# Gate and up products of two feed-forward blocks: the weights' high part times both parts of x in one product of 512 columns

## What is computed

```python
D_FF = 2816
def swiglu(x, w_gate, w_up, w_down):
    return (jax.nn.silu(x @ w_gate) * (x @ w_up)) @ w_down
...
    for l in range(DEPTH_2):
        h = x + 0.5 * swiglu(rms_norm_2(x, ffn1_norm[l]), ffn1_gate[l], ffn1_up[l], ffn1_down[l])
        u = rms_norm_2(h, mix_norm[l])
        ...
        h = h + jnp.concatenate([y_da, y_sc, y_lru], axis=-1) @ w_out[l]
        x = h + 0.5 * swiglu(rms_norm_2(h, ffn2_norm[l]), ffn2_gate[l], ffn2_up[l], ffn2_down[l])
```

## Time and profile before

| | |
|---|---|
| median of 3 runs | 1671.34 us (1671.28 to 1671.96) |
| the profiled execution | 1674.84 us, of which the span in the trace is 1673.0 us |
| instructions in the span | 26702 |
| PE busy | 1593.8 us, 95% of the span |
| DVE, ACT busy | 812.9 us (49%), 701.4 us (42%) |
| HBM traffic | 398.23 MB read, 239 GB/s over the span |

### The profile page before, as it was taken

The page is one execution under the profiler, slowest core; times in us unless marked ns, Lnnn a source line. Parts: engine busy times, 40 slices in busy tenths (PEclk is TensorE's granted clock), DMA queues, the critical chain, the costliest instruction groups (busy, mean ns, idle before and its releaser), DMA issues.

```text
span 1673.0 us, 26702 instructions
## 1 busy us (share of the span) xinstructions
PE 1593.8 (95%) x10902; PEld 1326.0 (79%) x10902; DVE 812.9 (49%) x1093; ACT 701.4 (42%) x760; POOL 47.0 (3%) x38
## 2 busy tenths in 40 slices
PE   7996879999999999999999999999999999999998
PEld 7895755555555554799999989999999989899997
DVE  4669631111111111465556766555665556766554
ACT  5564231212121212455445655343654454754443
POOL 0006300000000000000000000000000000000000
PEclk9898977878787878899999999999999999999999
DMA  7632489999999999766555336555555546346552
GB/s 232 182 101 76 157 338 429 427 428 429 428 428 429 428 428 429 250 205 196 177 176 176 127 124 220 184 180 171 187 193 176 194 132 205 123 153 200 182 194 75
DMA packets 164073, 400.19 MB, mean 239 GB/s; under 512 B 5752, under 2 KB 136232, under 8 KB 151592
## 3 DMA queue, kind: packets, MB, share of 16 engines
q1 hardware_dynamic: 162824, 397.74, 64.7%
q10 hardware_dynamic: 1184, 1.57, 0.3%
HBM read 398.23 MB, written 1.06 MB: 239 GB/s over the span
## 4 chain that ended last, share of the span: by engine, by line
PE 83%; DVE 6%; DMA 4%; ACT 3%; issue 2%; POOL 0%; SPq 0%; DVEq 0%; ACTq 0%; POOLq 0%
PE ps L573 13%; PE ps L575 12%; PE ps L574 12%; PE ps L806 11%; PE ps L598 6%; PE ps L599 6%; PE ps L600 6%; PE ps L794 5%; PE ps L814 5%; PE ps L855 3%; DMA ring<-w_in 2%; DMA ring<-w_expert_up 2%; ACT w1h_sb L1119 1%; DVE ring L1559 1%; DVE w1l_sb L1507 1%
## 5 line engine op out<-in xcount | busy, mean ns | idle before, releaser
L1789 DVE TENSOR_TENSOR wl_sb<-raw_sb,wh_sb 128x2048 fp32r<-128x2048 f32 x162 | 371.2, 2293 | 319.3 <-ACT wh_sb L1260 319.2
L573 PE MATMUL ps<-xTh_sb,wh_sb 128*128 128x256 f32 x1696 | 482.3, 284 | 5.7 <-DVE xTl_sb L1463 5.7
L575 PE MATMUL ps<-xTh_sb,wl_sb 128*128 128x256 f32 x1696 | 479.9, 283 | 0.0
L574 PE MATMUL ps<-xTl_sb,wh_sb 128*128 128x256 f32 x1696 | 479.8, 283 | 0.0
L1260 ACT ACTIVATE wh_sb<-raw_sb 128x2048 fp32r<-128x2048 f32 x162 | 310.5, 1916 | 308.7 <-PE ps L575 301.2
L573 PEld LDWEIGHTS ps<-xTh_sb,wh_sb 128*128 128x128 f32 x1696 | 325.2, 192 | 8.7 <-DVE xTl_sb L1463 7.1
L574 PEld LDWEIGHTS ps<-xTl_sb,wh_sb 128*128 128x128 f32 x1696 | 325.3, 192 | 1.5
L575 PEld LDWEIGHTS ps<-xTh_sb,wl_sb 128*128 128x128 f32 x1696 | 325.3, 192 | 0.0
L806 PE MATMUL ps<-ring,work 128*32 128x512 f32 x1152 | 156.0, 694 | 4.7 <-DMA ring<-w_expert_up 4.6
L598 PE MATMUL ps<-wh_sb,hidh_sb 128*128 128x512 f32 x384 | 151.2, 394 | 1.2 <-DVE wl_sb L1789 1.2
L599 PE MATMUL ps<-wl_sb,hidh_sb 128*128 128x512 f32 x384 | 149.9, 390 | 0.0
(11 more groups left out here) (305 smaller groups left out, 1850.6 us busy)
## 6 DMA issues: line engine op xcount, KB each, us to landing
ring<-w_expert_gate SPq DMA_DIRECT2D x24, 2048.0 KB, 20.8
ring<-w_expert_up SPq DMA_DIRECT2D x24, 2048.0 KB, 21.1
ring<-w_expert_down SPq DMA_DIRECT2D x24, 2048.0 KB, 27.2
raw_sb<-ffn_gate SPq DMA_DIRECT2D x44, 1024.0 KB, 5.4
raw_sb<-ffn_up SPq DMA_DIRECT2D x44, 1024.0 KB, 5.4
raw_sb<-ffn_down SPq DMA_DIRECT2D x44, 1024.0 KB, 4.8
raw_sb<-w_in SPq DMA_DIRECT2D x22, 1024.0 KB, 5.4
ring<-w_in SPq DMA_DIRECT2D x16, 1024.0 KB, 5.7
```

The source lines that it names most:

```text
L573: pe.matmul(to, w_h[:, k, fs], x_h[:, k, :], start=k == 0, stop=False)
L574: pe.matmul(to, w_h[:, k, fs], x_l[:, k, :], start=False, stop=False)
L575: mm = pe.matmul(to, w_l[:, k, fs], x_h[:, k, :], start=False, stop=k == KD - 1)
L1789: dve.tensor_tensor(wl[j], raw[j], wh[j].bitcast(F32), ALU.subtract).then_inc(raw_free[j], 1)
```

## The change

`xTh_sb` and `xTl_sb` become one tensor `xT_both`, high part first. For gate and up, `features3` is replaced by code in `weigh`: for each of the two feature blocks n and each k, one product w_h by (x_h, x_l) of 512 columns, which fills a whole bank, and one product w_l by x_h of 256 columns into that bank's first half. The second half of the bank holds w_h·x_l alone. Gate now takes banks 0 and 1, up banks 2 and 3, in every step: there is no double buffer by steps any more, and PE waits (semaphore `added`) until the step before has been read. ACT copies the banks' second halves out (`low`, 128x512 from PSUM into the free rows `f_low` of `xT_sb`), one copy ahead of each `hi`; DVE adds them to the first halves, one add (128x512) ahead of each `lo`. The two scalings by the rstd rows are then made from SBUF in place and both stand behind up's add. `rstd_rows` moves from bank 3 to bank 1, so it waits for gate(0)'s add, and gate's second feature block waits for `r_done`. Three semaphores of the first block are merged into one, `qk_stat`, to make room; its order stays. The mixer of the second block keeps `features3`.

```diff
+                    w_h, w_l = [by_cols(p) for p in parts(j, nth(L, f, r, s))]
+                    if fresh is None and not (r == UP and isinstance(s, int)):
+                        pe.wait_ge(sem["added"], 2 * q + 2 * s - 1 + r)
+                    for n in range(2):
+                        if fresh is None and r == GATE and n == 1:
+                            pe.wait_ge(sem["r_done"], 2 * L + f + 1)
+                        fs = slice(n * P, n * P + P)
+                        for k in range(KD):
...
+                            pe.matmul(bank(2 * r + n).rearrange("p (m s) -> p m s", m=2), w_h[:, k, fs], xT_hl[:, :, k, :],
+                                      start=k == 0, stop=False, skip_group_check=True)
+                            mm = pe.matmul(bank(2 * r + n)[:, 0:S], w_l[:, k, fs], xTh[:, k, :], start=False, stop=k == KD - 1,
+                                           skip_group_check=True)
...
+                    def low(r):
+
+                        act.wait_ge(*used_ffn(L, f, r, s))
+                        nc.scalar.activation(f_low[r], split(r)[:, :, 1, :], ACT.Copy).then_inc(sem["low_done"], 1)
+
+                    low(GATE)
                     if last:
-                        hi(f, nth_last(L, f), used_ffn(L, f, GATE, s))
+                        hi(f, nth_last(L, f))
...
+                        dve.wait_ge(sem["low_done"], 2 * q + 2 * s + 1)
+                        dve.tensor_tensor(gate, split(GATE)[:, :, 0, :], f_low[GATE], ALU.add).then_inc(sem["added"], 1)
                         lo(f if last else buf(f, GATE), n + i)
+                        dve.wait_ge(sem["low_done"], 2 * q + 2 * s + 2)
+                        dve.tensor_tensor(f_hid[c], split(UP)[:, :, 0, :], f_low[UP], ALU.add).then_inc(sem["added"], 1)
...
-                        dve.tensor_tensor(f_sil[c].rearrange("p (f s) -> p f s", f=2), bank(c).rearrange("p (f s) -> p f s", f=2),
-                                          rows(rstd_row), ALU.mult).then_inc(sem["gate_scaled"], 1)
...
+                        dve.wait_ge(sem["added"], 2 * q + 2 * s + 2)
+                        dve.tensor_tensor(gate, gate, rows(rstd_row), ALU.mult).then_inc(sem["gate_scaled"], 1)
+                        dve.tensor_tensor(f_hid[c], f_hid[c], rows(half_row), ALU.mult).then_inc(sem["up_scaled"], 1)
```

More of the change, by code:

```diff
@@ L313, in two_blocks, with split @@
         rstd_row, half_row, ones_p = xT[:, 0, :], xT[:, 1, :], xT[:, 2, 0:P]
+        f_low = [xT[:, 4 + 2 * r:6 + 2 * r, :] for r in range(2)]
+        def split(r):
+            return bank(2 * r, 2).rearrange("p (f m s) -> p f m s", f=2, m=2)
         raw, wh, wl = [[b[:, j * PIECE:(j + 1) * PIECE] for j in range(3)] for b in (raw_sb, wh_sb, wl_sb)]
@@ L321, in by_rows @@
             return w.rearrange("p (k n) -> p k n", n=D)
-        xTh, xTl = [b[:, :].rearrange("p (k s) -> p k s", k=KD) for b in (xTh_sb, xTl_sb)]
+        xT_hl = xT_both[:, :].rearrange("p (m k s) -> p m k s", m=2, k=KD)
+        xTh, xTl = xT_hl[:, 0, :, :], xT_hl[:, 1, :, :]
         hidh, hidl = [[b[:, 512 * c:512 * c + 512].rearrange("p (f s) -> p f s", f=2) for c in range(2)]
@@ L885, in rstd_rows @@
                     pe.wait_ge(sem["diag_dve"], 3 * L + 2 * f + 2)
+                    pe.wait_ge(sem["added"], 2 * q + 1)
                     for t in range(TT):
-                        mm = pe.matmul(bank(3)[:, t * P:t * P + P], ones_p, diag[:, t, :], start=True, stop=True)
+                        mm = pe.matmul(bank(1)[:, t * P:t * P + P], ones_p, diag[:, t, :], start=True, stop=True)
                     mm.then_inc(sem["r_ps"], 1)
@@ L898, in down @@
                         rows3((hidh[c], hidl[c]), w, [1], True).then_inc(done, 1)
-                weigh(0, 0, GATE, fresh)
-                weigh(0, 0, UP)
+                weigh(0, GATE, fresh)
+                weigh(0, UP)
                 rstd_rows()
                 with pe.Fori(0, STEPS // 2) as i:
-                    weigh(1, 2 * i + 1, GATE)
-                    pe.wait_ge(sem["r_done"], 2 * L + f + 1)
-                    weigh(1, 2 * i + 1, UP)
+                    weigh(2 * i + 1, GATE)
+                    weigh(2 * i + 1, UP)
                     down(0, 2 * i)
-                    weigh(0, 2 * i + 2, GATE)
-                    weigh(0, 2 * i + 2, UP)
+                    weigh(2 * i + 2, GATE)
+                    weigh(2 * i + 2, UP)
                     down(1, 2 * i + 1)
@@ L1182, in _ @@
             sqrt_table()
-            act.wait_ge(sem["qk_ms"], 1)
-            nc.scalar.activation(qk_std, qk_ms, ACT.Sqrt).then_inc(sem["qk_std"], 1)
+            act.wait_ge(sem["qk_stat"], SQUARED + 1)
+            nc.scalar.activation(qk_std, qk_ms, ACT.Sqrt).then_inc(sem["qk_stat"], 1)
             hi1(7)
@@ L1796, in step @@
                         i = 3 * s
-                        lo(f if last else buf(f, GATE), n + i)
-                        if not last:
-                            lo(buf(f, UP), n + i + 1)
                         hid = f_hid[c].rearrange("p f s -> p (f s)")
+                        gate = f_sil[c].rearrange("p (f s) -> p f s", f=2)
                         def rows(r):
```

40 lines of the change are left out of this document (22 added, 18 removed).

## The result

The changed kernel takes **1664.81 us** (median of 4 runs, 1662.98 to 1665.4 us) beside 1671.96 us of the kernel before on the same chip (5 runs, 1671.28 to 1672.63): a ratio of 0.9955 with an interval of 0.994 to 0.997. A fifth run of it took 5273.64 us, stands apart from all others and is left out. It is 7 us faster. 1655 was forecast, 16.6 us less; the time lies inside the range of 1645 to 1668, nearest to rival (a), and not half of the forecast gain is there. The profiled execution took 1664.78 us with a span of 1663.0 and a mean granted clock of 0.934.

What follows compares the result with a forecast made beforehand. PE's products were taken to bound the kernel. 18.4 us from cheaper pairs, minus 0.8 at the starts of halves and 1.0 after first halves, gave 16.6 us less: 1654.7, say 1655 us, range 1645 to 1668.

Steps and rivals of the forecast that it cites:

- rival (a): Gate and up: wide products run like the mixer's, 0.231 us each, pair 0.351, total 1660.6 us; chance 0.20.
- The pair: Gate and up: a wide plus a narrow product take 0.3467 us instead of 0.360, 1384 times, 18.4 us less.
- its sign of being wrong: The prediction is wrong if the step is not 0.4 us shorter, or PE is seen waiting in every step.
- Rival (d): Gate and up: each change of width costs, pair 0.364 us for 0.360, total 1678.2 us, slower; chance 0.08.
- (b): Gate and up: a 256 behind a 512 keeps the short 0.11 us, 30 us less, 1641; chance 0.08.
- (c): Gate and up: time above the columns grows with them, pair 0.360 us, nothing gained, total 1673.1; chance 0.09.
- The work of ACT and DVE in a step: In the new step of 16.55 us DVE has 10.8 and ACT 10.6 us of work; neither fills it.
- The lost double buffer: Gate and up: costs nothing, since gate(s+1) starts about 11 us after gate(s)'s end and its add is done 1.5 us after.
- The merged semaphores: First block: merging leaves its order unchanged and costs nothing.
- The start of a half: PE waits 0.2 us for `r_done` before gate(1)'s second block, four times, 0.8 us; bounds 0 and 0.5 each.
- The last step: After each layer's first half, ACT's later roundings delay table load and squares by 0.5 us, 1.0 in all; bounds 0 and 1.5.
- The rule: Opposing skill formula: a warm matmul takes N / 2.4 + 2.5 ns, so the change would save 1.7 us instead of 16.6.

Runs made afterwards that it cites:

- e4: The changed kernel with the low weights also multiplied by both parts of x, so every gate and up product has 512 columns: 1803.2 us, ratio 1.0782.
- e5: The changed kernel with each piece ordered wide, narrow, narrow, wide in runs of eight, except a half's first block: 1654.59 us, ratio 0.99.
- e1: The changed kernel with each feature block's eight products of 512 columns first, then its eight of 256: 1660.35 us, ratio 0.9925.
- e2: The changed kernel with x's high and low parts side by side for each k, making the wide operand one run: 1664.83 us, ratio 0.9955.
- e9: The changed kernel with neighbouring wide and narrow products in different PSUM banks, except a half's first piece: 1682.21 us in one run.
- e3: The changed kernel with its wide product split again into two of 256 columns, all else kept: 1672.37 us, ratio 0.9998.
- e6: The changed kernel with products in runs of two, wide k and k+1, then narrow k and k+1: 1655.05 us, ratio 0.9899.

## Why the prediction was right and wrong

**The pair, the step that failed.** 18.4 us rested on a pair of 0.2267 + 0.120 = 0.3467 us, "if each width keeps the distance that it has among its own kind". In the loop it takes 0.353, in the rhythm of 350, 361 and 349 ns: 32 x 0.0061 = 0.2 us and a `down` that is 0.04 longer (its first ten products, now behind a narrow one of a mixed row, are a little further apart) make 0.24 us a step, for 36 steps 8.7 us. With 0.5 for the slow stretches of the first steps that is 9.2 of the 18.4, and the trace has the other 9.2 as gain. The step is 0.19 shorter, and not 0.4, which the prediction named as its sign of being wrong. The two prices are right in themselves: e4 shows 0.2267 in this very loop, e5 0.2275, and e5's order of the same products gives the forecast time. What was mis-sized is the price of an order that no row of before had. From the five 512s behind 256s, 27 ns too long together, I argued that the loss fades and is no toll per change. It fades in a row of one width (e1, e5); behind `down`, one and one, it doesn't. But it is not so that turns can't reach the forecast price: six stretches of after run at 0.3467. So the forecast number does occur in the changed kernel, only not in the rows that start behind `down`, which are most of them. Rival (a), 0.351 and 1660.6, came nearest of the cases, but not by its reason: the mixer's 0.231 is of twelve products of 512 in a row, not of a mixture. Rival (d)'s 0.364 charged the whole loss of five products to each turn and was too high; (b) and (c) fell. The lower end of the range, said to be half-way to (b), would be 1648 by that rule and not 1645; nothing hangs on it.

**What is not settled.** Why one and one loses 6 ns a pair behind `down` and nothing behind some waits, runs of two about 1, and runs of four more than runs of two. The operand's form (e2), the bank (e9), the copies and adds (e3) and the wide product as such (e4) are out by experiment. That the loop's loss goes with the order of widths is shown (e1, e5, e6 change it and nothing else in the step); what in TensorE it acts on, and what puts a row into the one rhythm or the other, is not. A row of after made to start anew ahead of each gate piece was not tried.

**The work of ACT and DVE in a step.** Right: 10.76 us of DVE where 10.8 were forecast, no wait of PE on either, and e3 with the step of before. ACT has 9.04 us and not 10.6. The step of the earlier trace rows holds two table loads of 1.28 us and the one behind it none, with 6.86 us of work; after's step holds one. Nothing hung on it. The lost double buffer costs nothing that a step shows. The merged semaphores are of the first block, which no step shows; e3 has them too and is no slower than before.

**The start of a half.** 0.8 us were charged, four waits of 0.2 for `r_done`. In after ACT's timeline reads:

```profile
704.23 0.60 ACT L1292 ACTIVATE xT_sb<-ps 128x512 f32<-128x512 f32 x1 [2.69 <-PE ps L899]
704.72 1.91 ACT L1282 ACTIVATE wh_sb<-raw_sb 128x2048 fp32r<-128x2048 f32 x1
706.78 0.39 ACT L1305 ACTIVATE xT_sb<-ps 128x256 f32<-128x256 f32 x1
```

Copy, rounding and then the rstd rows, out at 707.17: the order and the durations that the prediction had. But PE's first block of gate(1) begins at 704.39, and its first wide product, behind the small ones, takes 0.09 us more than a later one, which the prediction left out (in before it is 0.21 for 0.12). With eight pairs at 0.353 PE comes to the second block at 707.30. The first pair behind the wait is 0.02 us longer than the others in the first half and 0.04 in the other three: 0.13 us, where 0.8 were charged. The slower pair explains only a part of that: in e5, whose first block runs at the forecast price, PE loses 0.08 us here, and not 0.2. What makes the fourth half 0.15 us longer from `rstd_rows` to `down` is not the wait, which is as long as in the second and third, but 22 pairs at 0.353 behind it for 0.3467.

**The last step.** 0.5 us twice were charged. ACT's timeline of after, with the earlier trace rows of before:

```profile
870.59 0.63 ACT L1311 ACTIVATE hidh_sb<-work 128x512 fp32r<-128x512 f32 x1 [0.83 <-DVE work L1848]
871.13 3.71 ACT L1282 ACTIVATE wh_sb<-raw_sb 128x2048 fp32r<-128x2048 f32 x2
874.86 1.28 ACT L1121 ACT_TABLE_LOAD   x1
...
876.26 1.01 ACT L1067 ACTIVATE xn_sb<-ps 128x1024 f32<-128x1024 f32 x1
```

and PE's, with the earlier trace rows:

```profile
866.77 0.40 PE L605 MATMUL ps<-wh_sb,hidh_sb 128*128 128x512 f32 x1
...
879.03 1.24 PE L533 MATMUL ps<-diag_sb,x_sb 128*128 128x128 f32 x9 [1.16 <-ACT diag_sb L1086]
```

The two roundings now stand back to back, and the turn comes 12.26 us behind the first of the 48 products of `down`, for 11.78: 0.48 us, as worked out. What the prediction left out is that 0.16 come back behind it: from the turn to the features 4.31 us for 4.47, since the second block of rows, which waits for the end of down(10) and not for ACT, is no later than before. Net 0.32, twice. e3 has the same 12.25 and, with the step of before, a time 0.2 us below it, so the whole of the edges is small. Down(10) was charged nothing at 0.3 us of cover, and PE runs its 48 products without a break.

**The rule.** In the long rows of before a product of 256 has 13.3 ns above its columns, and the sum went by that. The measured gain, 7 us or 8.3 by the two traces, lies between that sum and the 1.7 us by the Trainium skill, "TensorE: Matmul & The Clock Gate", section "Back-to-back issue gap". The trace doesn't bear out its fixed part of 2.5 ns: e5, without turns, gains 17.6 us, which a saving of 2.5 ns a product can't give. The section gives that formula for a product by itself; its other figure, 131 ns a product of 512 columns in a stream of weight loads and products, isn't met either, the row has 226.7. The page's section has a single width in view, and the loss seen here is one of two widths mixed.

## What to carry to other kernels

Where two products of different widths can be ordered freely, don't let them go one and one: one row of each width, with rows of the same width meeting (wide behind `down`, narrow behind narrow), was worth 10 us here for no instruction more, and runs of two, the smaller edit, as much (1655.05 and 1654.59 us). Price a merged product by a row of the trace that has the mixture and begins as it will in the loop, not by long rows of each width; where there is none, that term is the one to keep wide and to test first. Before an order is changed, see which wait rides on it: the same regrouping ahead of data that come in pairs (e1), or a wait moved ahead of a whole piece (e9), can take back a part of what the order brings, or more than all of it.

## What the runs showed of the hardware

- Products of 256 and 512 columns one and one take 0.353 us a pair behind a row of 512s, in a rhythm of 350, 361 and 349 ns, but 0.3467, the sum of their own prices, in six stretches behind a wait. In runs of two they take 0.348, of four 0.350, of eight and sixteen 0.348. With 1, 2, 4, 8 and 16 in a row the step is 16.79, 16.59, 16.69, 16.61 and 16.575 us: it doesn't fall evenly.
- A moving operand in two runs of 256 columns streams like one run (16.79 us both), and it doesn't matter whether both widths write one bank or two (16.79 and 16.80).
- In e9 a wait of PE of 2.6 us was followed by some 3.5 us at the lower clock level, 1.2 GHz, in three of four halves (1.8 us lost each; the granted clock of the 3.5 us behind the wait is 0.53, 0.63 and 0.65), and by a clock of 1.00 in the third, with the same wait ahead of it. In after the wait of 1.2 us at the start of the first half left the clock at 1.00; in e1, which then waits again between its wide products, it was 0.70 over 5 us in the first half and 1.00 in the third.
